# Convolution blocks in the order B, C, x, and a scan that starts group by group

## What is computed

```python
xbc = jax.nn.silu(causal_depthwise_conv(sxbc, conv_w, conv_b))
xs, bs, cs = jnp.split(xbc, [SSD_WIDTH, SSD_WIDTH + SSD_GROUPS * SSD_STATE], axis=-1)
...
cb = jnp.einsum("bclgn,bcsgn->bcgls", cc, bc)
y_diag = jnp.einsum("bcgls,bcgrls,bcsgrp->bclgrp", cb, decay_in, xd)
chunk_states = jnp.einsum("bclgn,bcgrl,bclgrp->bcgrpn", bc, decay_to_end, xd)
...
y = (y.reshape(B, S, SSD_WIDTH) * jax.nn.silu(sz.astype(F32))).astype(dtype)
y_ssd = rms_norm(y.reshape(B, S, SSD_GROUPS, gsz), ...)
```

## Time and profile before

| | |
|---|---|
| median of 3 runs | 3585.84 us (3581.7 to 3586.27) |
| the profiled execution | 3581.68 us |
| its span, first to last instruction | 3579.9 us |
| PE, DVE, ACT, POOL busy | 96%, 62%, 47%, 1% of the span |
| granted clock of PE, mean | 0.982 |
| read from HBM | 699.59 MB |

### The profile page before, as it was taken

One profiled execution on the slowest core, in us unless ns is written; L12 is line 12 of the kernel. 1 busy time (PEld: TensorE's weight loads), 2 busy tenths in 40 slices (PEclk: granted clock), 3 DMA queues, 4 the chain that ended last, 5 costly groups with the idle time before them and its releaser, 6 DMA issues. The chain is left out here.

```text
span 3579.9 us, 44702 instructions
## 1 busy us (share of the span) xinstructions
PE 3434.9 (96%) x18692; PEld 2957.1 (83%) x18692; DVE 2235.2 (62%) x2667; ACT 1691.2 (47%) x2088; POOL 33.8 (1%) x66
## 2 busy tenths in 40 slices
PE   5799999999999999999999999999999999999998
PEld 4679878778888887799888888888888789988887
DVE  5687666756667556676556576654566676654554
ACT  3355554454433344545644643333445775533333
POOL 0000000000000000000000000000000000000000
PEclk8799999999999999999999999999999999999999
DMA  8654455546777555444443367665554443455554
GB/s 344 265 205 163 167 190 216 198 163 245 270 261 280 214 183 191 155 165 154 153 153 142 137 232 270 250 241 199 182 187 178 167 169 137 159 215 188 188 188 153
DMA packets 100138, 708.80 MB, mean 198 GB/s; under 512 B 11776, under 2 KB 11808, under 8 KB 16224
## 3 DMA queue, kind: packets, MB, share of 16 engines
q1 hardware_dynamic: 93888, 675.38, 51.4%
q0 software_dynamic: 5472, 27.06, 2.2%
q10 hardware_dynamic: 576, 3.50, 0.2%
HBM read 699.59 MB, written 6.30 MB: 197 GB/s over the span
## 5 line engine op out<-in xcount | busy, mean ns | idle before, releaser
L1436 ACT ACTIVATE HH<-RAW 128x2048 fp32r<-128x2048 f32 x546 | 1044.9, 1914 | 1181.4 <-PE G L1184 882.4
L1790 DVE TENSOR_TENSOR LL<-RAW,HH 128x2048 fp32r<-128x2048 f32 x546 | 1248.0, 2287 | 350.6 <-ACT HH L1436 349.2
L1184 PE MATMUL G<-HH,UH 128*128 128x512 f32 x2560 | 1026.3, 401 | 64.8 <-DVE LL L1790 64.5
L1184 PE MATMUL G<-HH,UL 128*128 128x512 f32 x2560 | 1005.3, 393 | 0.0
L1184 PE MATMUL G<-LL,UH 128*128 128x512 f32 x2560 | 1005.3, 393 | 0.0
L1184 PEld LDWEIGHTS G<-HH,UH 128*128 128x128 f32 x2560 | 485.4, 190 | 183.8 <-DVE LL L1790 74.3
L1184 PE MATMUL G<-UH,HH 128*128 128x256 f32 x2080 | 605.4, 291 | 18.1 <-DVE XS L2038 10.0
L1184 PE MATMUL G<-UH,LL 128*128 128x256 f32 x2080 | 591.3, 284 | 0.0
L1184 PE MATMUL G<-UL,HH 128*128 128x256 f32 x2080 | 591.2, 284 | 0.0
L1184 PEld LDWEIGHTS G<-LL,UH 128*128 128x128 f32 x2560 | 485.1, 190 | 103.4
L1184 PEld LDWEIGHTS G<-HH,UL 128*128 128x128 f32 x2560 | 486.0, 190 | 99.9 <-issue 2.9
(11 more groups left out here) (335 smaller groups left out, 2421.0 us busy)
## 6 DMA issues: line engine op xcount, KB each, us to landing
RAW<-in_w_in_packed_dram SPq DMA_DIRECT2D x402, 1024.0 KB, 4.8
RAW<-w_ada_turned_packed_dram SPq DMA_DIRECT2D x88, 1024.0 KB, 4.9
RAW<-in_w_out_packed_dram SPq DMA_DIRECT2D x48, 1024.0 KB, 4.8
RAW<-in_w_o_ssd_packed_dram SPq DMA_DIRECT2D x32, 1024.0 KB, 4.8
RAW<-in_w_o_fox_packed_dram SPq DMA_DIRECT2D x16, 1024.0 KB, 4.9
RAW<-in_w_o_dsa_packed_dram SPq DMA_DIRECT2D x16, 1024.0 KB, 4.8
RAW<-in_w_proj_a_packed_dram SPq DMA_DIRECT2D x16, 1024.0 KB, 4.8
RAW<-in_w_proj_b_packed_dram SPq DMA_DIRECT2D x16, 1024.0 KB, 4.8
```

The costliest lines, as they stand in the source:

```text
L1184: mm = pe.matmul(to, lt, rh, start=first, stop=end, skip_group_check=True)
L1436: a.activation(HH[g % NH][:, :n], RAW[buf(ch["f"])][:, :n], ACT.Copy).then_inc(*hi_done.up(g))
L1790: v.tensor_tensor(LL[buf(f)][:, :n], RAW[buf(f)][:, :n], HH[g % NH][:, :n].bitcast(F32), ALU.subtract).then_inc(*lo_done.up(g))
```

## The change

The six convolution blocks come in the order B, C, x0, x1, x2, x3 (`CONV_BLOCKS`). Tiles follow each other in that order (`CONV_BEFORE`); the last x tile's turn gets a step of its own. The scan is put into the side lane after the first x block, and group g waits in the plan until tile 4g + 3 has been turned. Instructions are the same in number and shape on PE and DVE.

```diff
+CONV_BLOCKS = (4, 5, 0, 1, 2, 3)
+CONV = [j * 4 + i for j in CONV_BLOCKS for i in range(4)]
+CONV_BEFORE = dict(zip(CONV[1:], CONV))
...
     def conv(l, jb):
+        def turn(ct):
+            put("conv_turn", l, ct)
+            ended("conv_putd", l, ct)
+
         def steps(b):
             for ct in range(jb * 4, jb * 4 + 4):
                 o.tok_block["conv", l, ct] = b
                 put("conv", l, ct)
-                if 0 < ct <= 20:
-                    put("conv_turn", l, ct - 1)
-                    ended("conv_putd", l, ct - 1)
+                if ct in CONV_BEFORE and CONV_BEFORE[ct] < 20:
+                    turn(CONV_BEFORE[ct])
                 if ct % 4 == 3:
                     o.blocks[b]["free_by"] = ("conv_silu", l, ct)
-                if ct == 23:
-                    ended("conv_bc", l, ct)
+                yield
+            if ct == CONV[-1]:
+                turn(ct)
                 yield
...
     def ssd(l):
         for g in range(4):
+            while ("conv_turn", l, 4 * g + 3) not in o.evac_before:
+                yield
...
-        conv_b = [o.wblock(w, SX + j * 512, conv(l, j), u_ready) for j in range(6)]
         o.ssd_prog[l] = [{"done": False} for _ in range(4)]
-        o.side.add(o.when(conv_b, ssd(l)))
+        for n, j in enumerate(CONV_BLOCKS):
+            conv_b = o.wblock(w, SX + j * 512, conv(l, j), u_ready)
+            if n == 2:
+                o.side.add(o.when([conv_b], ssd(l)))
...
-            if ct < 2:
-                a.wait_ge(*evac_before("conv", l, 0))
-            elif ct < 18:
-                a.wait_ge(*conv_turned.at(l, ct - 2))
+            if ct in CONV[:2]:
+                a.wait_ge(*evac_before("conv", l, CONV[0]))
             else:
-                a.wait_ge(*conv_bc.at(l, ct - 2))
+                y_before = CONV_BEFORE[CONV_BEFORE[ct]]
+                a.wait_ge(*(conv_turned if y_before < 16 else conv_bc).at(l, y_before))
```

## The result

| | before | after |
|---|---|---|
| median of four runs, us | 3586.06 (3581.7 to 3587.49) | 3636.89 (3630.69 to 3643.24) |
| profiled execution, us (its span) | 3581.68 (3579.9) | 3636.47 (3634.7) |
| mean granted clock of TensorE | 0.982 | 0.976 |

A forecast was written before the change was run, and what follows sets the result against it. PE, busy 96% of the span, was taken as the bound, so only its waits could move time, chiefly for DVE's low weight half (LL). Terms summed to 53.4 us, plus 10 of clock: together +63, forecast 3647 us, range 3616 to 3672.

The forecast's parts named there:

- Part 1: Eight head blocks: scan halves share slots with norm parts, so PE waits; 17.0 us in layer 1, 16.7 in layer 0.
- Part 2: Scan beside the convolution's last block: PE waits there; 5.4 us in layer 1, 5.0 in layer 0.
- Part 3: Scan beside the gated block `dg`: PE waits there; 2.4 us in layer 1, 4.7 in layer 0.
- Part 4: `fox` attention five slots earlier, leaving the turn of `sz` uncovered; 1.9 us in layer 1, 4.9 in layer 0.
- gains: Chunk 79's 2.8 us wait goes, and 0.9 us a layer of PE's wait for ACT's attention-weights copy; -4.6 us.
- B and C tiles beside `ix_top`: Convolution tiles beside `ix_top`: said to change nothing, since DVE is late there and does the same work.
- clock: Granted clock falls behind some 16 new waits of 2 us or longer, every second costing 1.7; +10 us, between 0 and 20.
- (a): Rival: waits at the product in the middle of a chunk do not add; 3598 to 3615, chance 0.09.
- (b): Rival: faster, since attention leaves chunks 89 to 92, chunk 79's wait goes and ACT hides decays; 3573, chance 0.04.
- (c): Rival: the scan's steps fit into slack, lo being early in half of chunks 249 to 270; 3583 to 3592, chance 0.03.
- (d): Rival: worse than summed, layer 0 waits push dots and buffer releases, clock falls each time; 3672 to 3700, chance 0.05.
- (e): Rival: a table switch costs twice its 1.28 us row where ACT has just worked; 32 us more, 3679, chance 0.02.

The follow-up runs named there:

- d4: The changed kernel with the scan held back four steps of its lane instead of none; 3631.9 us, ratio 1.0122.
- only1: The changed kernel with the scan held back five steps in layer 0 alone, so the change takes effect in layer 1 only; 3616.4 us, ratio 1.0074.
- both filled runs: The changed kernel with 14 idle matmuls before PE's wait for DVE's multiply, in seven places or in layer 1 alone; 3636.4 and 3636.7 us.
- halves first: The changed kernel with each half of the scan's exponentials put ahead of the head-block norm part in its slot; 3612.0 us, ratio 1.0071.

## Why the prediction was right, and where its terms were wrong

The forecast was 3647 (3616 to 3672), slower; measured 3636.9. The reason for the sign held: PE's work is the same, so only its waits and the clock could move the time, and the halves of the scan meet the norms. But the sum was right only by luck, because two errors nearly cancel: the waits were predicted at 53 us and are 30, the clock at 10 and is 27. The low end of the range does not fit its own rule either: the sum less a quarter and no clock is 3626, not 3616; the result lies above both.

| term | predicted | measured |
|---|---|---|
| Part 1, layer 1 | 17.0 | 7.1 (1.44; 1.69; 0.35 + 2.38; 0.34 + 2.38, less the 1.5 of the earlier trace rows) |
| Part 1, layer 0 | 16.7 | 5.6 (1.79; 2.87; 0.34 + 4.09; 2.64, less 6.1 of before) |
| Part 2, layer 1, layer 0 | 5.4, 5.0 | 4.9, 2.3 |
| Part 3, layer 1, layer 0 | 2.4, 4.7 | 2.4, 2.6 |
| Part 4, layer 1, layer 0 | 1.9, 4.9 | 2.0, 5.2 |
| gains | -4.6 | -4.6 |
| not in the sum: B and C tiles beside `ix_top`, chunks 92 and 93 | 0 | 2.1 |
| clock | +10 | +27 |

**The step that failed in Part 1** is the one that puts ACT's load of the exponential's table behind DVE's copy and add ("ACT loads the exponential's table (1.28) and runs four exponentials"). The fence of after shows the load at 1810.97, the moment the root is out, while DVE scales, copies and adds until 1812.8: the load does not wait for what its instruction waits for, and only 0.59 us are left to wait. The second load stands at 1819.15, and DVE's add runs beside it:

```profile
1819.41 0.68 DVE L2295 TENSOR_TENSOR WW<-BD,CST 128x512 f32<-128x512 f32 x1
```

By these rows the overlap takes 1.3 us out of the first chain (the add's end at 1812.81 and a load behind it, against exponentials at 1812.84) and 0.9 out of the second (1820.09 and a load, against 1820.45). That is 2.2 of the 2.6 us between the 5.3 predicted for a block and the 2.7 that chunks 255 and 259 show. The earlier trace rows could not tell: there DVE's add was over by 1713.42, before ACT came to the load at 1714.62. But the same trace has a row that could have. In layer 0 ACT loads the same table and then sits for DVE's add:

```profile
480.93 1.28 ACT L1712 ACT_TABLE_LOAD   x1
483.68 1.28 ACT L1712 ACTIVATE WW<-WW,T4T 128x128 f32<-128x128 f32 x4 [1.47 <-DVE WW L2283]
```

The first of the two head waits, LL, was predicted at 1.8 and is 0.35 for this reason (at chunk 251 there is none); the product's at 3.5 and is 2.38, and 1.69 in chunk 251. At 243, where no table is switched, the count was right: 2.65 and 2.3 predicted, 2.39 and 1.96 measured; so at chunk 271 (1.5 and 0.9; 1.55 and 0.83), and for the turned tile in chunk 286 (2.02).

**In layer 0** the same error stands in each block. Besides, the product's wait that I put behind each LL wait is absent or nearly so in chunks 46 (0.37), 54, 62 and 74: PE came 2.4 to 3.8 us late to the chunk, and the multiply was ready or nearly so. The tiles beside `ix_top`, said to change nothing, cost 0.9 us of waits a layer.

**The clock.** The term took 1.7 us for every second wait over 2 us. Measured: 34 us of half clock in layer 1 and 44 in layer 0, where 3.4 and 20 stood. Behind the waits of 2.4 us in chunks 255 and 259 stand 6.8 us each time, worth 3.4, twice the price that I had taken from the earlier trace rows. And it falls behind shorter waits than those I counted. The number was off the other way: 16 new waits of 2 us or more were expected, and the two stretches have 15 where 6 stood. So the mis-sized term is the price of one wait.

**The rivals.** (a) fell: the waits in the middle of a chunk are there and add. (b) and (c) fell by the time alone: it is neither faster nor within 3583 to 3592. (d) was the right direction for the clock, not for the waits. (e) fell: at 1819.15 the load is followed by the exponentials after 1.30 us, and with 16 of its 103 loads taken from the kernel before the time did not move (3586.4). The Trainium skill, page "ScalarE: Activation LUTs", section "What ACT_TABLE_LOAD costs", puts 1.38 us of drain beside each load; by it the four loads of the first long fence would add some 5.5 us to ACT's chain, an estimate from that page. The traces don't show it.

What I should have asked is not only how long two chains are in one slot, but which of them can start first. The rival that the halves, ahead of the norm, hide wholly (as they do in layer 1: no wait in four blocks) stood nowhere.

## What to carry to other kernels

When a change puts two pieces of work into one slot of in-order queues, look at what each waits for: the one whose input is already there goes first, and the other's wait hides it; the same work the other way round cost 26 us here. Count the meetings for every position of the moved work, not for one: six positions, one step apart, cost from nothing to 52 us. And price the clock as well as the wait: over the two stretches 29.6 us of new waits came with 27.3 us of clock, though a single wait of 1.4 to 2.4 us cost between nothing and 3.4.

## What the runs showed of the hardware

- ACT starts a table load while the instruction that needs it still waits for another engine (load at 1810.97, DVE's add until 1812.8, exponentials at 1812.84). In the kernel before, with 1.47 us of waiting left behind such a load at 480.93, the switch cost nothing.
- Behind PE's waits of 2.38 us for the product in chunks 255 and 259 the granted clock fell to 0.5, 1.2 GHz, for 6.8 us in all three kernels that have them (after, d4, only1). Behind the wait of 1.69 us in chunk 251 it fell in after (6.8 us) and not in d4 and only1; behind the 1.44 to 1.46 us in chunk 247 it fell for 3.4 us in after and only1, not in d4. In only1, behind chunk 251's wait:

```profile
1764.00:1769.00 5.00, 5.00 (x29) 4.05 (x29) 4.16 (x4) 0.62 (x1) 0.00 (x0) 1.00 0.00 0
```

  and in after:

```profile
1788.00:1793.00 5.00, 4.83 (x20) 3.70 (x21) 2.51 (x3) 1.19 (x1) 0.00 (x0) 0.62 0.00 0
```

  The same wait in the same code can cost 0 or 3.4 us of clock. The wait of 2.02 us ahead of chunk 290 has 3.4 us of half clock behind it in before and only1 and none in after.
- With matmuls that nobody needs in front of the wait, the clock stayed at 1.00 in these places, and the run as a whole was no faster.
- The granted clock also fell where PE had not waited: three pieces of 3.4 us in chunks 274 to 280 of both filled runs, two in chunks 278 and 280 with halves first, with PE busy throughout.
